# A hybrid decoder layer on 8 cores: the first tile through fp32 rows, and two weight pieces loaded in the tile before

## The chip, the cores and the metric

The kernel runs on the 8 NeuronCores of one Trainium2 chip. Each core runs the same program on its own sequence. The time is that of the device in microseconds, and the slowest core sets it. TensorE is called PE here, VectorE DVE, ScalarE ACT, GpSimd POOL, and SyncE, which only issues transfers, SP.

## The reference, cut to what matters

```python
def layer(x, c, conv_prev, g_mix, w_ada, b_ada, w_in, g_v, w_s, b_s, w_conv, w_out, g_ffn, w_ff1, w_ff2):
    mod = jax.nn.silu(c) @ w_ada + b_ada                          # (B, 6*D)
    sh1, sc1, gt1, sh2, sc2, gt2 = [m[:, None, :] for m in jnp.split(mod, N_MOD, axis=-1)]
    h = rmsnorm(x, g_mix) * (1.0 + sc1) + sh1
    p = h @ w_in                                                   # (B, T, D_IN)
    u, v, bg, cg, hin = jnp.split(p, [D_A, 2 * D_A, 2 * D_A + D_B, 2 * D_A + 2 * D_B], axis=-1)
    u = jax.nn.gelu(u)
    v = rmsnorm(jax.nn.gelu(v).reshape(bsz, t, N_HEADS_A, HEAD_DIM_A), g_v.reshape(N_HEADS_A, HEAD_DIM_A))
    a_out = u * chunk_spatial_mix(v, w_s, b_s).reshape(bsz, t, D_A)
    y_conv, new_conv = short_conv(cg * hin, conv_prev, w_conv)     # width 3, causal
    b_out = bg * y_conv
    mix = jnp.concatenate([a_out, b_out], axis=-1) @ w_out
    x = x + gt1 * mix
    h2 = rmsnorm(x, g_ffn) * (1.0 + sc2) + sh2
    f = jnp.square(jax.nn.relu(h2 @ w_ff1)) @ w_ff2
    return x + gt2 * f, v.reshape(bsz, t, D_A), new_conv
```

D_MODEL is 1024, D_A and D_B are 512, D_FF is 4096. There are 8 prompt sequences of 2048 rows and 128 single sample rows. All inputs are fp32. A core has one prompt sequence and 16 sample rows.

## The kernel before, in words

A core takes its 2048 rows in 8 tiles of 256 rows. Phase A (`tA`, the token mixer) runs over the tiles t0 to t7 and writes the new rows to a scratch tensor `x1_scr` in device memory; phase B (`tB`, the MLP) reads them back tile by tile. All weights are converted to bf16 by their transfers, which POOL issues (1024 KB in SBUF each, twice that in device memory). They are `w_ada` in 12 pieces (`ada_dma(q)`), `w_in` in the 5 groups u, v, C, h, B (`win_dma`), `w_out` in two, `w_ff1` and `w_ff2` in 8 pieces each (`ff1_dma(p)`, `ff2_dma(p)`). Rows of x and everything small are moved by transfers that SP issues. No scheduler is in play. The helper class `Sched` only records operations and adds the semaphore waits that the buffers need, so that each engine and each queue works in exactly the order in which the code is written. An engine that waits holds up all that stands behind it.

A tile of phase A goes through these steps.
- `n_load` fetches two blocks of 128 rows into buffers of the array `X`. `n_stats` squares them on ACT with a running sum, DVE scales it, and POOL takes the power of -1/2. `n_mod` multiplies the rows by that factor and by `g1B`, which is the row g_mix*(1+sc1) repeated on all partitions. `n_tr` transposes the bf16 result on PE, and ACT copies it to `hT`.
- `A_u`, `A_v` and `conv` (with `A_ch` and `A_b`) are the products with `w_in`. `A_vn` normalises v on DVE after POOL's power, and `A_spatial` is the mix within the chunk.
- `A_wout` is the product with `w_out`, four matmul groups (j, n) for a tile. DVE multiplies each by `gt1B` into one of two buffers `tmpx`, and POOL adds that onto x, which `A_reload` has fetched once more into `X[xr]`, `X[xr+1]`. SP then stores the rows to `x1_scr` (semaphores `x1s_i_j`, for tile i and block j).

The matmul results go to 8 PSUM banks, of which `next_bank` hands out 7 in turn; a bank comes free when the engine that reads it is done.

The set-up computes the modulation: `ada_cols(q)` is a product with one piece of `w_ada`, and `ada_bcast` spreads a half of sc1 over all partitions through fp32 matmuls (line 374) to make `g1B`. `setup_spatial` builds small constants on POOL and DVE and has SP copy two of them (the transfers arena<-arena). The tiles t0 to t2 are interleaved by hand in the set-up; `A_u_hold` leaves the results of u in banks until the bias is known. `wst` holds `w_s`, which POOL masks and `setup_spatial_pe` transposes. From t3 on `steady(i, mid, end, nxt, nn)` writes out a tile. It does the output products of an earlier tile `mid` before conv and of another, `end`, after it: steady(4) has t1 and t2, steady(5) has t3 and t4, steady(6) has t5, steady(7) has t6. Between the steps, `ex()` takes the next job from the list `pending`.

Several buffers of the first tiles lie where pieces 4 to 7 of `w_ff1` go later. The place of piece 4 holds X[4] and X[5], that of piece 6 holds `aT` 2 and 3 and `bT` 3 (`aT` and `bT` are the two inputs of `A_wout`).

## Time and profile before

| what | us |
|---|---|
| median of 3 runs (783.75 to 789.23) | 787.66 |
| the profiled execution, device time | 784.98 |
| its span on the slowest core, core 4 | 783.4 |
| the span of core 6, the next longest | 783.2 |
| the spans of the eight cores | 776.2 to 783.4 |
| PE busy on core 4 | 721.9 (92%) |
| PE busy in the first 92 us of core 4 | 49.86 |

The profiled execution is 1.6 us longer than the span of its slowest core and 2.7 us shorter than the median. Phase A with its set-up ends at about 313 us of the span, and the eight tiles of phase B fill the rest. Times below are microseconds from the start of the span on core 4. In the rows, a line number of a helper stands for many operations: L317 is any group of matmuls from `mm_group`, L325 any `tensor_tensor`, L328 any `scalar_tensor_tensor`, L322 any activation and L99 any transfer.

### The profile page before, as it was taken

The numbers are of one execution on the slowest core, as the hardware profiler recorded it, in microseconds if no ns is written. First come the engines' busy times: TensorE is split into PE (matmuls) and PEld (weight loads), VectorE is DVE, ScalarE is ACT, GpSimd is POOL, SyncE is SP. The second block draws the span as 40 slices with busy tenths as digits, with TensorE's granted clock in tenths as the row PEclk, the third lists the DMA queues.
The fourth block names the chain that finished last, engine by engine and source line by source line (L and its number), as shares of the span: only waits on it lengthen the run. The fifth ranks groups of instructions, "written<-read, shape, count | busy, mean of one in ns | idle before, by whom it ended". The sixth has DMA issues, their size and how long they took to land.

```text
span 783.4 us, 16529 instructions; the slowest of 8 cores (776.2 to 783.4 us)
## 1 busy us (share of the span) xinstructions
PE 721.9 (92%) x5941; PEld 498.7 (64%) x5976; DVE 373.3 (48%) x795; ACT 272.5 (35%) x560; POOL 141.8 (18%) x154
## 2 busy tenths in 40 slices
PE   1468799999999999997999999999999999999996
PEld 0354477767575766843784784774874865865854
DVE  0333667665757675440643444434433543533523
ACT  2234335423332332441441451351441531532511
POOL 5213302434544453110010000000000000000000
PEclk9989799999999999999999999999999999999998
DMA  9999999999998859997110100200200200200001
GB/s 143 186 172 168 185 187 139 172 197 247 194 275 191 201 96 208 179 192 126 67 44 26 70 18 28 82 2 28 82 1 28 82 2 27 82 1 28 28 1 55
DMA packets 46983, 83.03 MB, mean 106 GB/s; under 512 B 2204, under 2 KB 31654, under 8 KB 46902
## 3 DMA queue, kind: packets, MB, share of 16 engines
q0 software_dynamic: 32304, 36.70, 34.1%
q1 hardware_dynamic: 14598, 45.27, 18.4%
q8 instruction: 49, 0.80, 0.4%
q14 instruction: 32, 0.26, 0.1%
HBM read 101.73 MB, written 16.96 MB: 151 GB/s over the span
## 4 chain that ended last, share of the span: by engine, by line
PE 79%; DMA 14%; DVE 2%; issue 2%; ACT 1%; POOL 1%; another core or an unknown queue 0%; DVEq 0%; POOLq 0%; ACTq 0%; SPq 0%
PE ps L317 71%; DMA arena<-w_ff 6%; DMA arena<-w_ada 6%; DMA arena<-w_s 3%; PE ps L438 1%; PE ps L890 1%; ACT arena L322 1%; DVE arena L328 1%; DVE arena L325 1%; PE ps L746 1%; PE ps L583 1%; PE ps L579 1%; POOL arena L99 1%; PE ps L350 1%; PE ps L656 1%
## 5 line engine op out<-in xcount | busy, mean ns | idle before, releaser
L317 PE MATMUL ps<-arena 128*128 128x256 bf16 (+3 forms) x4376 | 635.0, 305 | 10.4 <-DVE arena L325 3.6
L317 PEld LDWEIGHTS ps<-arena 128*128 128x128 bf16 x4408 | 430.1, 98 | 205.0 <-issue 23.1
L325 POOL TENSOR_TENSOR arena<-arena 128x1 f32<-128x1 f32 (+3 forms) x100 | 107.1, 1076 | 597.1 <-DVE arena L398 466.6
L325 DVE TENSOR_TENSOR arena<-arena 128x256 bf16<-128x256 f32 (+8 forms) x354 | 159.5, 459 | 113.6 <-ACT arena L322 102.3
L322 ACT ACTIVATE arena<-ps,arena 128x256 f32<-128x256 f32 (+1 forms) x320 | 147.1, 472 | 137.4 <-PE ps L317 74.3
L322 ACT ACTIVATE arena<-arena 128x256 f32<-128x256 f32 (+4 forms) x101 | 76.8, 772 | 204.9 <-DVE arena L325 143.3
L325 DVE TENSOR_TENSOR arena<-ps,arena 128x512 f32<-128x512 f32 (+6 forms) x98 | 59.4, 610 | 179.4 <-PE ps L317 129.1
L328 DVE SCALAR_TENSOR_TENSOR arena<-arena 128x256 f32<-128x256 f32 (+4 forms) x118 | 96.2, 822 | 22.6 <-POOL arena L325 15.6
L322 ACT ACTIVATE arena<-ps 128x1024 bf16<-128x1024 bf16 (+4 forms) x86 | 50.6, 590 | 158.3 <-PE ps L438 92.1
L328 DVE SCALAR_TENSOR_TENSOR arena<-ps,arena 128x256 bf16<-128x256 f32 (+1 forms) x64 | 31.0, 484 | 23.2 <-PE ps L317 11.2
L890 PE MATMUL ps<-arena 128*128 128x512 bf16 x125 | 28.4, 379 | 5.6 <-DMA arena<-w_ff 4.8
L438 PE MATMUL ps<-arena 128*128 128x128 bf16 x256 | 20.2, 231 | 6.4 <-DVE arena L328 5.8
L890 PEld LDWEIGHTS ps<-arena 128*128 128x128 bf16 x128 | 12.0, 97 | 21.5 <-issue 8.0
L438 PEld LDWEIGHTS ps<-arena 128*128 128x128 bf16 x256 | 17.3, 103 | 9.6 <-issue 7.4
L398 DVE TENSOR_SCALAR arena<-arena 128x1 f32<-128x1 f32 x46 | 7.0, 153 | 33.1 <-ACT arena L322 32.4
L521 DVE TENSOR_REDUCE arena<-arena 128x8 f32<-128x512 f32 x16 | 10.9, 682 | 11.4 <-ACT arena L322 11.4
L350 PE MATMUL ps<-arena 128*128 128x17 bf16 x384 | 11.8, 172 | 4.9 <-DMA arena<-w_ada 4.9
L350 PEld LDWEIGHTS ps<-arena 128*128 128x128 bf16 x384 | 11.6, 98 | 5.7 <-issue 5.3
L99 POOL DMA_DIRECT2D arena<-w_ff x16 | 13.4, 840 | 9.2 <-PE ps L317 7.2
L99 POOL DMA_DIRECT2D arena<-w_ada x12 | 11.3, 941 | 10.8 <-PE ps L350 9.8
L374 PE MATMUL ps<-arena 128*128 128x128 f32 x16 | 4.1, 437 | 8.4 <-DVE arena L995 7.1
L579 PE MATMUL ps<-arena 34*128 34x512 bf16 x16 | 6.6, 412 | 5.0 <-DVE arena L1022 5.0
(86 smaller groups left out, 106.9 us busy)
## 6 DMA issues: line engine op xcount, KB each, us to landing
arena<-x_p SPq DMA_DIRECT2D x32, 512.0 KB, 11.4
arena<-w_ff POOLq DMA_DIRECT2D x16, 1024.0 KB, 36.2
arena<-w_ada POOLq DMA_DIRECT2D x12, 1024.0 KB, 44.4
x_scr<-arena SPq DMA_DIRECT2D x16, 512.0 KB, 9.6
arena<-x_scr SPq DMA_DIRECT2D x16, 512.0 KB, 4.2
y_p<-arena SPq DMA_DIRECT2D x14, 512.0 KB, 2.9
arena<-w_in POOLq DMA_DIRECT2D x5, 1024.0 KB, 64.4
arena<-w_out POOLq DMA_DIRECT2D x2, 1024.0 KB, 88.3
```

The lines of the kernel that those rows point to most:

```text
L99: fn = lambda eng, o=out, i=in_: eng.dma_start(out=o, in_=i)
L317: ins = e.matmul(out, lhsT=l, rhs=r, start=(first and i == 0), stop=(last and i == n - 1))
L322: S.op("act", lambda e: e.activation(out=out, in_=in_, func=func, **kw), reads=reads, writes=writes)
L325: S.op(eng, lambda e: e.tensor_tensor(out=out, in0=in0, in1=in1, op=op), reads=reads, writes=writes)
L328: S.op("dve", lambda e: e.scalar_tensor_tensor(out=out, in0=in0, scalar=scalar, in1=in1, op0=op0, op1=op1), reads=reads, writes=writes)
L350: ins = e.matmul(bk[:, cc * 17:(cc + 1) * 17], lhsT=ff1_v[s][:, k, cc * 128:(cc + 1) * 128], rhs=siluCT3[:, k, :], start=(k == 0), stop=(k ...
L438: ins = e.transpose(psb[:, (k - k0) * 128:(k - k0 + 1) * 128], hb[:, k * 128:(k + 1) * 128], identb)
L521: S.op("dve", lambda e: e.tensor_reduce(out=ss, in_=sqv.rearrange("p (h d) -> p h d", h=8), axis=AX.X, op=ALU.add), reads=[sqv_b], writes= ...
L579: e.matmul(bk[:, :], lhsT=indK[0:34, :], rhs=bsK[0:34, :], start=True, stop=False, skip_group_check=True)
L583: ins = e.matmul(bk[p0:p0 + 64, (h // 2) * 128:(h // 2 + 1) * 128], lhsT=vt[:, h * 64:(h + 1) * 64], rhs=wmT3[:, h, :], start=False, stop= ...
L656: ins = e.matmul(bk[:, gi * 64 + c * 16:gi * 64 + (c + 1) * 16], lhsT=w_in_g[nm][:, k, c * 128:(c + 1) * 128], rhs=hsT3[:, k, 0:16], start ...
L890: ins = e.matmul(bk[:, :], lhsT=f3[:, k, j * 128:(j + 1) * 128], rhs=wff2_v[:, k, n * 512:(n + 1) * 512], start=(k == 0), stop=(k == 31))
```

## The change

Four things are changed.

First, t0 goes another way. Its rows are multiplied in fp32 by their own factor on ACT (`first_rows`), transposed in fp32 on PE (`first_tr`, 16 transposes into 4 banks), and multiplied by g_mix*(1+sc1) when they leave the banks, where this factor is a value per partition (`first_scale`, half of it on DVE and half on ACT). t0 so needs no `g1B`.

Second, the set-up is written in another order. Both `ada_bcast` come after `ada_cols(3)`, `setup_spatial` comes after them, w_s is loaded before t2 and g_v after it without a wait, the steps n_stats and n_mod of t2 come before `ada_cols(0)`, the masking and `setup_spatial_pe` come before `ada_cols(1)`, and `ada_dma(6)` and `(7)` come after A_v of t2. A Gelu on one column is put behind the Silu.

Third, `A_v` is recorded as two operations: its 8 big matmuls no longer wait for the bias row `vbK`, only the ninth does.

Fourth, the buffers `aT` and `bT` of t4 to t7 are numbers 1, 0, 1, 0 (before 1, 2, 3, 0), and the rows of t4 are reloaded into X[2] and X[3] (before X[4] and X[5]), in steady(5) after the output product of t3 instead of before it. Pieces 6 and 4 of `w_ff1` are fetched in steady(5) (before: piece 4 in steady(6), piece 6 in steady(7)).

```diff
@@ A_v
-        S.op("pe", mm_group(bk[:, :], [(h3[:, k, j * 128:(j + 1) * 128], w_in_g["v"][:, k, :]) for k in range(8)]
-                            + [(onesK[0:34, :], vbK[0:34, :])]),
-             reads=[htb, win_b["v"], onesK_b, vbK_b], writes=[bkb])
+        S.op("pe", mm_group(bk[:, :], [(h3[:, k, j * 128:(j + 1) * 128], w_in_g["v"][:, k, :]) for k in range(8)], last=False),
+             reads=[htb, win_b["v"]], writes=[bkb])
+        S.op("pe", mm_group(bk[:, :], [(onesK[0:34, :], vbK[0:34, :])], first=False), reads=[onesK_b, vbK_b], writes=[bkb])
@@ AI: the number of aT and bT
-        return (tl["i"] + 1) % 4
+        return (1, 2, 3, 0, 1, 0, 1, 0)[tl["i"]]
@@ tA
-    ... xr=(4, 2, 4, 2, 4, 2, 2, 2)[i],
+    ... xr=(4, 2, 4, 2, 2, 2, 2, 2)[i],
@@ set-up
+    act(bF[:, 0:1], mhalf[:, 0:1], AF.Gelu_apprx_tanh, [mhalf_b], [bF_b[0]])
...
-    for j in range(2):
-        n_stats(tA[0], j)
-    setup_spatial()
+    def first_rows(tl):
+        for j in range(2):
+            n_stats(tl, j)
+        for j in range(2):
+            xt, xb, _ = X[tl["x"] + j]
+            rs, rs_b = tl["rs"][j]
+            act(xt, xt, AF.Copy, [xb] + rs_b, [xb], scale=rs)
+    XT_BANKS = (5, 6, 7, 2)
+    def first_tr(tl):
+        for q, b in enumerate(XT_BANKS):
+            bk, bkb = banks[b]
+            def fn(e, bk=bk, q=q):
+                ins = None
+                for kk in range(2):
+                    for j in range(2):
+                        k = 2 * q + kk
+                        ins = e.transpose(bk[:, kk * TILE + j * 128:kk * TILE + (j + 1) * 128], X[tl["x"] + j][0][:, k * 128:(k + 1) * 128], identf)
+                return ins
+            S.op("pe", fn, reads=[X[tl["x"]][1], X[tl["x"] + 1][1], identf_b], writes=[bkb])
+    def first_scale(tl, hf):
+        h3, htb = h3_of(tl)
+        m, mb = modT[1]
+        bk, bkb = banks[XT_BANKS[2 * hf + 1]]
+        k0 = 4 * hf + 2
+        tt("dve", h3[:, k0:k0 + 2, 0:TILE], bk.rearrange("p (k t) -> p k t", k=2), m[:, k0:k0 + 2, 16:17].broadcast_to([128, 2, TILE]),
+           ALU.mult, [bkb, mb], [htb])
+        bk, bkb = banks[XT_BANKS[2 * hf]]
+        for kk in range(2):
+            k = 4 * hf + kk
+            act(h3[:, k, 0:TILE], bk[:, kk * TILE:(kk + 1) * TILE], AF.Copy, [bkb, mb], [htb], scale=m[:, k, 16:17])
+    ring[0] = (0, 1)
+    first_rows(tA[0])
     ada_cols(2)
-    ada_bcast(2, g1B, g1B_b, col, col_b)
+    first_tr(tA[0])
+    first_scale(tA[0], 0)
...
     ada_cols(3)
+    first_scale(tA[0], 1)
+    ada_bcast(2, g1B, g1B_b, col, col_b)
     ada_bcast(3, g1B, g1B_b, col, col_b)
     q3_in = landed(ff1_b[ADA_SLOT[3]])
-    q1_in = landed(ff1_b[ADA_SLOT[1]])
-    for j in range(2):
-        n_mod(tA[0], j)
+    setup_spatial()
@@ loads of the set-up and t0 to t2
     for j in range(2):
         n_load(t1, j, after=[q3_in])
+    load(wst3, w_s.rearrange("h t s -> t h s"), wst_b, "wst", after=[win_b["u"]])
     for j in range(2):
-        n_load(t2, j, after=[win_b["u"]])
-    load(gvB, g_v.partition_broadcast(128), [gvB_b], "gvB", after=[q1_in])
-    load(wst3, w_s.rearrange("h t s -> t h s"), wst_b, "wst")
-    for j in range(2):
-        n_tr(t0, j)
+        n_load(t2, j)
+    load(gvB, g_v.partition_broadcast(128), [gvB_b], "gvB")
     A_u_hold(t0, hold[0])
...
@@ steady
-        if end is not None:
+        if end is not None and i < 5:
             reload(end)
...
         if mid is not None:
             wout(mid)
+        if end is not None and i == 5:
+            reload(end)
@@ pending
-        lambda: s_v2(),
+        lambda: (s_v2(), ff1_dma(6)),
...
-        lambda: s_zout(ncs[:, 512:1024].rearrange("t (c n) -> t c n", c=4)),
+        lambda: (s_zout(ncs[:, 512:1024].rearrange("t (c n) -> t c n", c=4)), ff1_dma(4)),
...
-        lambda: ff1_dma(4),
+        None,
         lambda: s_mod(x1sT, x1sT_b, 4, 3),
-        None, None,
-        lambda: ff1_dma(6),
```

Where the instructions now stand can be seen in three places.

DVE in the set-up, the changed kernel from the set-up's second `ada_cols` on (L325 with 128x68 and L328 belong to it, L325 with 128x512 is the second half of `first_scale`, the two L367 are the columns of the two `ada_bcast`, L965 to L970 are `setup_spatial`):

```order
L325 TENSOR_TENSOR arena<-ps1,arena 128x68 [waits c_pe,c_act]
L328 SCALAR_TENSOR_TENSOR arena<-arena 128x68 [waits c_dve]
L325 TENSOR_TENSOR arena<-ps2,arena 128x512 [waits c_dve]
L367 COPY arena<-arena 128x512
L367 COPY arena<-arena 128x512 [waits c_dve,c_pe]
L965 CAST arena<-arena 2x128 [waits c_pool]
L967 CAST arena<-arena 2x512 [waits d_bsrow,c_pool]
```

Before, the casts L965 to L970 stood ahead of both `ada_cols` on DVE; now they stand behind the second column copy, which waits for PE.

SP in the set-up, before and after as one piece (x_p are rows of t1 and then of t2; d_ff1w1 is piece 3 of `w_ada`, d_ff1w3 piece 1; ahead of this piece stand the two copies of `setup_spatial`, arena<-arena, each with a wait for DVE, in both kernels):

```order
 L99 DMA arena<-x_p 128x1024 [waits d_ff1w1]
 L99 DMA arena<-x_p 128x1024
-L99 DMA arena<-x_p 128x1024 [waits d_win_u,d_X0,c_act,c_dve]
-L99 DMA arena<-x_p 128x1024 [waits d_X1,c_act,c_dve]
-L99 DMA arena<-g_v 128x512 [waits d_ff1w3]
-L99 DMA arena<-w_s 128x8x128
+L99 DMA arena<-w_s 128x8x128 [waits d_win_u]
+L99 DMA arena<-x_p 128x1024 [waits c_act,c_pe]
+L99 DMA arena<-x_p 128x1024 [waits c_act]
+L99 DMA arena<-g_v 128x512
```

w_s moved ahead of t2 and away from the wait for piece 1 of `w_ada`; the loads of t1 kept their place behind the two copies.

SP in steady(5) and steady(6), before and after as one piece (x_p with a wait for x1s_i_j is a reload that waits until the store of tile i, block j has landed; x1_scr<-arena are the stores of t3 and further down of t4):

```order
-L99 DMA arena<-x_p 128x1024 [waits d_x1s_2_0]
-L99 DMA arena<-x_p 128x1024 [waits d_x1s_2_1]
 L99 DMA x1_scr<-arena 128x1024 [waits c_pool] x2
+L99 DMA arena<-x_p 128x1024 [waits d_x1s_3_0]
+L99 DMA arena<-x_p 128x1024 [waits d_x1s_3_1]
 L99 DMA ncs<-arena 16x4x128 [waits c_dve]
 L99 DMA mod_scr<-arena 8x128 [waits c_dve]
 L99 DMA x1_scr<-arena 128x1024 [waits c_pool] x2
-L99 DMA arena<-x_p 128x1024 [waits d_x1s_3_0]
-L99 DMA arena<-x_p 128x1024 [waits d_x1s_3_1]
+L99 DMA arena<-x_p 128x1024 [waits d_x1s_4_0]
+L99 DMA arena<-x_p 128x1024 [waits d_x1s_4_1]
```

The reload of t4 now stands behind the stores of t3 and waits for them, and that of t5 waits for the stores of t4 instead of those of t3.

## Rows read from the trace of the kernel before

**Rows 1.** The page: clock and DMA share in tenths, 40 slices of the span.

```profile
PEclk9989799999999999999999999999999999999998
DMA  9999999999998859997110100200200200200001
```

**Rows 2.** Chain that ended last, first 140 us: start, length, what.

```profile
6.14 44.50 DMA arena<-w_ada
...
51.09 20.74 DMA arena<-w_s
```

**Rows 3.** Timeline of the first 135 us: start, length, engine, line [idle before <-releaser].

```profile
21.32 3.41 SPq L99 DMA_DIRECT2D arena<-arena  x2
24.83 10.44 SPq L99 DMA_DIRECT2D arena<-x_p  x4
29.47 2.04 PE L374 MATMUL ps<-arena 128*128 128x128 f32 x8 [1.34 <-DVE arena L367]
37.45 5.81 PE L317 MATMUL ps<-arena 128*128 128x256 bf16 x32 [1.43 <-ACT arena L322]
46.08 3.65 PE L317 MATMUL ps<-arena 128*128 128x256 bf16 x32 [1.93 <-ACT arena L322]
67.93 8.45 PE L317 MATMUL ps<-arena 128*128 128x512 bf16 x35 [1.94 <-DVE arena L325]
82.70 0.58 PE L579 MATMUL ps<-arena 34*128 34x512 bf16 x1 [4.98 <-DVE arena L1022]
85.29 6.23 PE L317 MATMUL ps<-arena 128*128 128x512 bf16 x17 [0.33 <-issue]
131.66 0.96 PE L350 MATMUL ps<-arena 128*128 128x17 bf16 x32
```

**Rows 4.** Stretches of 2 us, PE alone: busy, instructions, clock, DMA share, GB/s.

```profile
76.00:78.00 2.00, 1.72 (x12) 1.00 1.15 158
80.00:82.00 2.00, 0.00 (x0) 0.50 1.18 170
```

**Rows 5.** Transfer of piece 6 of w_ada: its issue, then us to landing.

```profile
73.00 1.80 POOL L99 DMA_DIRECT2D arena<-w_ada  x2
...
arena<-w_ada POOLq DMA_DIRECT2D x1, 1024.0 KB, 54.7
```

**Rows 6.** Stores of t3, the adds before them, and DVE in t5, t6.

```profile
225.11 2.97 SPq L99 DMA_DIRECT2D x_scr<-arena  x2
242.04 0.69 DVE L325 TENSOR_TENSOR arena<-ps,arena 128x512 f32<-128x512 f32 x1 [1.10 <-PE ps L317]
258.48 0.69 DVE L325 TENSOR_TENSOR arena<-ps,arena 128x512 f32<-128x512 f32 x1 [1.17 <-PE ps L317]
255.78 1.26 POOL L325 TENSOR_TENSOR arena<-arena 128x512 f32<-128x512 f32 x1 [3.62 <-DVE arena L325]
```

**Rows 7.** Us to landing: stores of 225.1, 258.9; loads of 247.3, 297.8, 216 to 218.5.

```profile
x_scr<-arena SPq DMA_DIRECT2D x1, 512.0 KB, 11.0
x_scr<-arena SPq DMA_DIRECT2D x1, 512.0 KB, 5.2
arena<-x_p SPq DMA_DIRECT2D x1, 512.0 KB, 7.7
arena<-x_p SPq DMA_DIRECT2D x1, 512.0 KB, 9.9
arena<-x_p SPq DMA_DIRECT2D x1, 512.0 KB, 14.6
```

**Rows 8.** Stretches of 10 us: busy of PE, PEld, DVE, ACT, POOL; clock, DMA share, GB/s.

```profile
240.00:250.00 10.00, 10.00 (x106) 5.33 (x105) 7.00 (x9) 2.46 (x4) 7.02 (x5) 1.00 0.76 180
280.00:290.00 10.00, 9.95 (x66) 5.96 (x65) 6.71 (x12) 3.66 (x7) 8.62 (x8) 1.00 0.38 49
```

**Rows 9.** Waits of PE, 130 to 420 us: core 4, then core 6.

```profile
PE ps L890 <- DMA arena<-w_ff: 4.8, 3, 2.6
...
PE ps L890 <- DMA arena<-w_ff: 4.1, 2, 2.3
```

More of the change, by code:

```diff
@@ L900, in build_nc @@
     NT = SEQ // TILE
-    tA = [dict(kind="A", i=i, w=TILE, row0=i * TILE, x=(2 if i in (1, 3) else 0), h=(0, 1, 2, 0, 1, 0, 1, 0)[i], xr=(4, 2, 4, 2, 4, 2, 2, 2)[i],
+    tA = [dict(kind="A", i=i, w=TILE, row0=i * TILE, x=(2 if i in (1, 3) else 0), h=(0, 1, 2, 0, 1, 0, 1, 0)[i], xr=(4, 2, 4, 2, 2, 2, 2, 2)[i],
                x1b=bufs("x1s_%d_0" % i, "x1s_%d_1" % i)) for i in range(NT)]
@@ L1035, in build_nc @@
     hold = {0: (3, 4), 1: (5, 6)}
-    ring[0] = (0, 1, 2, 7)
     for j in range(2):
         n_load(t1, j, after=[q3_in])
+    load(wst3, w_s.rearrange("h t s -> t h s"), wst_b, "wst", after=[win_b["u"]])
     for j in range(2):
-        n_load(t2, j, after=[win_b["u"]])
-    load(gvB, g_v.partition_broadcast(128), [gvB_b], "gvB", after=[q1_in])
-    load(wst3, w_s.rearrange("h t s -> t h s"), wst_b, "wst")
-    for j in range(2):
-        n_tr(t0, j)
+        n_load(t2, j)
+    load(gvB, g_v.partition_broadcast(128), [gvB_b], "gvB")
     A_u_hold(t0, hold[0])
+    ring[0] = (0, 1, 2, 7)
     for j in range(2):
@@ L1052, in build_nc @@
     A_u_hold(t1, hold[1])
+    for j in range(2):
+        n_stats(t2, j)
+    S.op("pool", lambda e: e.affine_select(out=wst3, in_=wst3, compare_op=ALU.is_ge, fill=0.0, base=0,
+                                           pattern=[[0, 8], [-1, 128]], channel_multiplier=1), reads=wst_b, writes=wst_b)
+    for j in range(2):
+        n_mod(t2, j)
     ada_cols(0)
@@ L1055, in build_nc @@
     for j in range(2):
-        n_stats(t2, j)
-    for j in range(2):
-        n_mod(t2, j)
-    for j in range(2):
         n_tr(t2, j)
-    S.op("pool", lambda e: e.affine_select(out=wst3, in_=wst3, compare_op=ALU.is_ge, fill=0.0, base=0,
-                                           pattern=[[0, 8], [-1, 128]], channel_multiplier=1), reads=wst_b, writes=wst_b)
+    setup_spatial_pe()
     ada_cols(1)
@@ L1072, in build_nc @@
         A_u(t2, c)
-    for q in (6, 7):
-        ada_dma(q)
     load(xS, x_s.rearrange("t (k n) -> (t k) n", k=8), [xS_b], "xS", after=[win_b["C"]])
@@ L1086, in build_nc @@
         A_v(t1, j)
-    setup_spatial_pe()
     for j in range(2):
@@ L1093, in build_nc @@
         A_v(t2, j)
+    for q in (6, 7):
+        ada_dma(q)
     for j in range(2):
```

## The prediction

> **What bounds the kernel now.** Start with the page [rows 1]: the clock row shows two dips, in slices 3 and 5 (about 40 to 100 us), and the DMA row stands at 9 for the first 12 slices, to 235 us. PE is busy 49.86 of the first 92 us and nearly all the time afterwards. So only three places are left where an edit of order can gain: the set-up, the point where phase A ends, and whatever wait the change itself makes. I read them in that order.
>
> In the set-up, the chain of waits [rows 2] names the transfer of the last early piece of `w_ada` (to 50.6 us) and then w_s, which SP issues at 51.09, only after that piece, and which lands at 71.8. The timeline [rows 3] shows what hangs on it: the spatial product of t0 starts at 82.70 after PE has waited 4.98 us. That wait takes the clock along: it is 1.00 at 76 us and 0.50 (1.2 GHz of 2.4) at 80 us [rows 4]. The 17 matmuls of A_v(t2) behind it take 6.23 us, where 17 at the rate of the 35 before it (8.45 us) would take 4.1 [rows 3]: 2.1 us is this trace's price of one such cold stretch.
>
> At the end of phase A, PE waits 4.8 us in three waits for pieces of `w_ff2` on core 4, and 4.1 on core 6 [rows 9]. There the transfers are late, not PE.
>
> Between 100 and 340 us PE hardly waits. Nothing is to be won there; whatever the change adds there is lost. The DMA share is 1.0 to 1.1 until 240 us, then 0.76, and 0.38 at 280 to 290 us [rows 8]: there is some room late in phase A, and it is into this room that the two pieces of `w_ff1` are moved.
>
> **The set-up.** t0 no longer waits for `g1B`, but both `ada_bcast` still stand ahead of its u product on PE. Piece 3 lands at about 24 us; `ada_cols(3)`, which now stands behind the 16 fp32 transposes, ends near 26; DVE then scales, copies the first column at 28, PE takes 2.04 us for each cast [rows 3], the second copy waits for the first cast, and the second cast ends near 33. A_u_hold(t0) starts there instead of 37.45 [rows 3]: 4.5 us won at this point.
>
> What is lost stands on SP. The two copies of `setup_spatial` are issued at 21.32 and 24.15, the rows of t1 at 24.83 [rows 3]. These copies need DVE casts which now stand behind the second column copy, so near 31.5 and 34. The loads of t1 are queued behind them and leave at about 34.7, 10 us later, and w_s, t2 and g_v follow in one heap. With the 9.9 us that a load takes on full DMA queues [rows 7], t1 is there at 44.6 and 46.5. Squares, power, `n_mod` (1.28 us a block) and transposes add 6 to 7 us, and A_u_hold(t1) starts near 53 instead of 46.08, cold again, since PE had 10 us with nothing to do: 5.8 us instead of 3.65 [rows 3]. Through t2, `ada_cols(1)` and the bias of u, I come to A_v(t0) at 71.5, 3.6 us later than 67.93; 1.9 of what it would be later is given back because A_v no longer waits for `vbK` (its wait there is 1.94 [rows 3]), and 1.3 by the table load that is now done early.
>
> From there the order pays. A_v of t0 and t1 takes 8.45 us, to 80. The mask, the transposes of w_s and the copy at line 1022 are done long before; the power for t0 is no longer queued behind two `ada_dma`. The spatial product of t0 waits for v alone and starts near 80.3, 0.4 us after A_v(t1), too little to lose the clock. 1.4 us for it and 4.1 for A_v(t2) give 85.8 instead of 91.5: 5.7 us ahead.
>
> Not all of it survives. Piece 6 of `w_ada` is issued at 73.0 and lands 54.7 us later, at 127.7 [rows 5]; its product starts at 131.66 [rows 3]. Transfers issued by POOL are served in order, and the bytes ahead of this piece are the same in the changed kernel, so PE cannot be more than 4.0 us ahead there. **Term 1: -4.0 us.** Its bounds are 0 (t1 and t2 land 5 us later than I think) and -4.8 (less other traffic ahead of piece 6).
>
> **The end of phase A.** Piece 6 of `w_ff1` is issued at 291 us today, in the middle of the pieces of `w_ff2`; it lands after 25.4 us and takes some 10 us of the queue. Moved to steady(5), it frees these 10 us, while PE needs the last pieces only 4.8 earlier: all waits go. What is late next is PE itself. On core 4 that is 4.8 us, but core 6 (span 783.2) waited 4.1 [rows 9], and 783.2 - 4.1 = 779.1 is the slowest core then. **Term 2: -4.3 us**, with bounds of 0 and -4.8.
>
> **Tiles 5 and 6.** This is the part that costs. t4's rows used to be fetched into X[4] and X[5], free long before. Now X[2] is taken: t3's sum must be added, stored and landed before t4 can be fetched, and t5 comes behind t4 in the same buffer. In times of the kernel before: the store of t3 is issued at 225.1 and lands 11.0 us later [rows 6, 7], at 236.1. The reload then takes 9.9 (a load on full queues) or 7.7 (at share 0.76) [rows 7, 8]. The queues will be full: two more pieces stand ahead, and a piece takes 10 us or more there, so the room after 240 us is used up until about 275. I take 9.9: t4 is there at 246.0.
>
> POOL needs 1.26 us for an add [rows 6]. DVE has two buffers `tmpx`, so its third multiply of t4 waits for the first add, to 247.3 instead of 242.04 [rows 6]. PE does not feel this: the banks that it needs next are free. But the store of t4 can only go at 248.7. With 11.0 and 9.9 once more, t5 is there at 269.6, its first add ends at 270.9, and the third multiply of t5, at 258.48 today [rows 6], ends at 271.6. Behind it on DVE stands the whole of conv(t6). PE has five small groups after its output product of t5 (the square sum of the sample rows, a transpose, C, H, C), to about 263.3; the sixth needs the bank that the third multiply reads. PE stands still from 263.3 to 271.7, 8.4 us, which is longer than the 4.98 that brought the clock down in the set-up, so I add the same 2.1. SP, too, waits with the loads of tB[0] behind the reload of t5; ACT squares these late in conv(t6), with 1 us to spare or short of it. **Term 3: +10.5 us.** Its lower bound is nothing: with 5.2 for a store and 7.7 for a load the third multiply of t5 would not be held beyond 262. Its upper bound uses 14.6, the slowest class of load [rows 7], for both loads: t4 at 250.7, t5 at 279.0, the multiply done at 281, a stall of 17.7 and with the clock 19.8.
>
> One rule of the Trainium skill bears on this ("DMA: Bandwidth & Descriptors", section on queues, rings and completion order): each DMA engine takes packets in turn from the queues that have work. By it, a longer heap of weight pieces would not make a single reload slower, only the time of full queues longer. That is how I use 9.9 and 11.0, and the first of these rows was taken with `w_ff2` pieces in the heap.
>
> **Edits that cost nothing.** aT and bT in turns of two: t5 writes number 0 after the output product of t3 has read it, earlier on the same engine. The early issue of pieces 6 and 4 costs POOL nothing new. The fp32 transposes (3.5 to 4.3 us cold, an estimate from the 2.04 us of four fp32 products) are hidden while piece 3 is on its way; without that cover they would cost this much.
>
> **Sum.** -4.0 - 4.3 + 10.5 = +2.2 us. The profiled execution (784.98, its span 783.4) would become 787.2; the median, 2.7 above it, 787.66 + 2.2 = **789.9 us**.
>
> **Rivals.**
> The reload chain is hidden. If transfers are served faster, or the earlier pieces are through before 250 us, term 3 falls to 0 to 4. For it: at 247 us loads landed in 7.7, at 258.9 a store in 5.2 [rows 7]. Against it: these rows are from the room that the change fills. Time: 787.66 - 8.3 = 779.4 at best, 781 as its middle. Chance 0.24.
> The front gains nothing. The late rows of t1 and t2 eat all of the 5.7 us. For it: 10 us of delay at SP are sure from the order of instructions. Against: the wait at 82.70 and the cold stretch go for certain. Time: 793.9. Chance 0.12.
> The pieces of `w_ff2` stay late, so that moving piece 6 does not do what it is for, because they are issued late themselves (three at 313 us and after). Against: they land one after the other 5 to 10 us apart, as in a heap. Time: 794.2. Chance 0.05.
> The slow end: one mechanism, the chain of store, reload, add, store, reload for t3, t4 and t5. It decides from the point at which both legs together take more than about 16 us each round (the forecast has 20.9); at 25.6 the stall is 17.7 and the sum 19.8 - 8.3 = +11.5: 799 us, or 797 as its middle. For it: burst loads at 216 us took 14.6 [rows 7]. Chance 0.13.
>
> **How the numbers follow.** The forecast holds 0.46 and reaches from 785 to 794. A change of 1% (7.9 us) is about what a measurement of this kernel can tell from none. Below 779.8 lies half of the first rival, 0.12. Above 795.5 lies most of the slow end and a little of the second and third, 0.15. Between them 0.73. The range, 780 to 797, leaves out half of the first rival and a part of the last.
>
> **What the profile after would show.** Right: A_u_hold(t0) at about 33 us; rows of t1 issued on SP near 35 and a gap of PE near 40 to 49 us; no wait at the spatial product of t0 and the clock at 1.00 there; the product with piece 6 of `w_ada` near 127.7; no waits for `w_ff2`; a gap of PE of 6 to 10 us in conv(t6), ended by DVE, which was held by POOL, which waited for x_p. Wrong: if the rows of t1 are issued near 25, if no gap stands in conv(t6), or if stores and reloads in tiles 5 and 6 land within 7 us, the gain is larger than I say; if a second gap stands behind the reload of t4 in tile 5, it is smaller.

## The result and the profile after

The changed kernel takes 793.9 us (median of 6 runs, 793.06 to 798.79); the kernel before, run beside it, 785.85 (6 runs, 783.48 to 789.23). The ratio is 1.0108, with a 95% interval of 1.0084 to 1.0132: 8.5 us slower (1.08% of 787; the two medians differ by 8.05). The forecast was 2.2 us slower, or 789.9 us from a kernel before at 787.66. Some executions fall in a slower state of the chip, in which the cores of one die or both show a lower granted clock; medians, ratios and differences here are over the others alone. The profiled execution of after is the slowest of its six (798.79 us), so single waits in it may be longer than usual. Its cores span 786.5 to 797.2 us, with granted clocks of 0.967 to 0.977; before they were 0.982 to 0.987.

The page of after, the rows that answer [rows 1]:

```profile
span 797.2 us, 16579 instructions; the slowest of 8 cores (786.5 to 797.2 us)
...
PEclk9966999999899999999999999999999999999998
DMA  9999997999999938998030020200200200200001
```

Before, the clock stood at 8 in slice 3 and 7 in slice 5; now it is 6 in slices 3 and 4 (40 to 80 us): more of the set-up is cold, not less. A shallow dip is at slice 11 (about 200 us).

**The set-up.** Timeline of after, core 2, first 100 us, PE; the columns are start, length, engine, line, form and count, then the idle time before and what ended it. Answers to [rows 3]:

```profile
31.06 5.67 PE L317 MATMUL ps<-arena 128*128 128x256 bf16 x32
47.38 1.01 PE L438 MATMUL ps<-arena 128*128 128x128 bf16 x8 [10.65 <-DVE arena L328]
...
51.33 5.75 PE L317 MATMUL ps<-arena 128*128 128x256 bf16 x32 [1.32 <-ACT arena L322]
56.91 0.96 PE L350 MATMUL ps<-arena 128*128 128x17 bf16 x32
62.86 1.01 PE L438 MATMUL ps<-arena 128*128 128x128 bf16 x8 [4.99 <-DVE arena L328]
65.41 1.01 PE L438 MATMUL ps<-arena 128*128 128x128 bf16 x8 [1.54 <-DVE arena L325]
...
71.68 16.25 PE L317 MATMUL ps<-arena 128*128 128x256 bf16 x76
88.25 0.37 PE L579 MATMUL ps<-arena 34*128 34x512 bf16 x1 [0.31 <-issue]
...
97.84 1.75 PE L465 MATMUL ps<-arena 128*128 128x2 bf16 x64
```

Read it downwards. A_u_hold of t0 starts at 31.06 instead of 37.45 (near 33 was forecast). It runs cold: its 32 products take 5.67 us, where the same 32 take 3.65 at full clock (46.08 in [rows 3]). Then PE waits 10.65 us for the rows of t1 (L438 is the transposes) and 4.99 more for those of t2. The spatial product of t0 (L579) has lost its wait of 4.98, but comes at 88.25 instead of 82.70. The last row, the bias products of C and h, is my mark for the end of the set-up: 97.84 here, 96.8 to 99.5 over the cores; before it stood at 90.3 to 92.7 (91.4 in the mean, against 98.1). **The set-up is 5 to 7 us longer**, where 5.7 less were forecast at this point and 4.0 less behind piece 6 of w_ada. The loss stays: the product with piece 6 starts at 136.87 on core 2 (near 127.7 was forecast, 131.66 before on core 4), and the first L621, a small product of the sample rows, at 148.98, against 143.77 before on core 4.

Why t1 and t2 are late can be read in SP's queue, core 2, same columns:

```profile
29.27 2.73 SPq L99 DMA_DIRECT2D arena<-arena  x2
32.10 0.86 SPq L99 DMA_DIRECT2D arena<-x_p  x2
33.05 0.57 SPq L99 DMA_DIRECT2D arena<-w_s  x1
33.78 6.79 SPq L99 DMA_DIRECT2D arena<-x_p  x2
```

The two copies of `setup_spatial` go out at 29.3 instead of 21.3, and t1 behind them at 32.1 instead of 24.8 [rows 3]. Between t1 and t2 stands w_s. The transfers issued in these rows, us from issue to landing (w_s, then the first block of t2), and ACT's first square of t2:

```profile
arena<-w_s SPq DMA_DIRECT2D x1, 512.0 KB, 22.1
arena<-x_p SPq DMA_DIRECT2D x1, 512.0 KB, 23.4
57.33 1.06 ACT L322 ACTIVATE arena<-arena 128x1024 bf16<-128x1024 f32 x1 [6.15 <-DMA arena<-x_p]
```

w_s has the bytes of a block of x, in rows of 512 bytes instead of 4096, and takes 22 us; the block of t2 queued behind it takes 23.4 where the two of t1, ahead of w_s, take 10.9 in the median and 9.9 was forecast. The clock, in stretches of 2 us of core 2 (busy time of PE, PEld, DVE, ACT, POOL; clock; DMA share; GB/s), answering [rows 4]:

```profile
44.00:46.00 2.00, 0.00 (x0) 0.00 (x0) 0.40 (x2) 1.15 (x2) 0.45 (x2) 0.50 1.12 178
52.00:54.00 2.00, 2.00 (x11) 1.43 (x10) 0.00 (x0) 0.00 (x0) 0.00 (x0) 0.50 1.10 279
72.00:74.00 2.00, 2.00 (x12) 1.23 (x11) 0.74 (x5) 1.53 (x4) 0.00 (x0) 0.50 1.20 178
```

PE fell to 1.2 GHz in the wait for t1, and again in the one for t2, so that A_u of t2 too begins cold.

**Tiles 5 and 6.** The chain that ended last, core 2 (start, length, what), is the one that the prediction drew:

```profile
233.10 11.21 DMA x_scr<-arena
244.37 12.04 DMA arena<-x_p
259.30 8.85 DMA x_scr<-arena
268.20 7.65 DMA arena<-x_p
278.19 3.23 PE ps L317 x16
```

Store of t3, reload of t4, store of t4, reload of t5, then PE. POOL and PE in the timeline (POOL of core 2, PE of core 2, PE of core 6):

```profile
275.99 8.17 POOL L325 TENSOR_TENSOR arena<-arena 128x512 f32<-128x512 f32 x5 [7.95 <-DMA arena<-x_p]
278.19 3.23 PE L317 MATMUL ps<-arena 128*128 128x256 bf16 x16 [3.06 <-DVE arena L325]
275.32 3.26 PE L317 MATMUL ps<-arena 128*128 128x256 bf16 x16 [6.07 <-DVE arena L325]
```

The gap in conv(t6) is there on four cores (2, 3, 0 and 6: 3.06, 3.12, 4.10 and 6.07 us), and on the other four not at all.

**The end of phase A.** No core of after waits for w_ff2; the first products with it (L890) run through on core 2 (against 4.8 and 4.1 us of waits in [rows 9]):

```profile
357.28 25.23 PE L890 MATMUL ps<-arena 128*128 128x512 bf16 x112
```

**One thing that no step spoke of.** On cores 1, 2, 3, 4 and 7 PE pauses in tile 4, amid the short products of the sample rows (L656), with nothing to wait for, and runs on cold. Core 2:

```profile
201.58 0.39 PE L656 MATMUL ps<-arena 128*128 128x16 bf16 x9 [4.20 <-issue]
201.82 7.35 PE L317 MATMUL ps<-arena 128*128 128x256 bf16 x48
```

The same 48 products take 5.40 us on core 6, which has no pause. In the profiled execution of before no core has it.

### The profile page after: what moved, and what is told of

Its sections match the earlier page's. It is cut to its first block, busy times and chain, and to the rows that moved or that the text cites. A ratio compares the mean times of both kernels' runs of the same rounds, so it can differ in the third digit from the quotient of the medians.

```text
span 797.2 us, 16579 instructions; the slowest of 8 cores (786.5 to 797.2 us)
## 1 busy us (share of the span) xinstructions
PE 731.6 (92%) x5976; PEld 503.4 (63%) x5976; DVE 370.9 (47%) x795; ACT 274.9 (34%) x565; POOL 142.9 (18%) x154
## 4 chain that ended last, share of the span: by engine, by line
PE 68%; DMA 16%; DVE 4%; issue 4%; POOL 3%; ACT 2%; SPq 1%; DVEq 0%; POOLq 0%; ACTq 0%
PE ps L317 60%; DMA arena<-x_p 11%; DMA x_scr<-arena 4%; POOL arena L325 3%; PE ps L890 3%; ACT arena L322 2%; DVE arena L325 2%; DVE arena L328 2%; SPq L99 1%; DMA mod_scr<-arena 1%; PE ps L438 1%; PE ps L746 1%; PE ps L1009 0%; PE ps L465 0%; DVE arena L521 0%
## 5 line engine op out<-in xcount | busy, mean ns | idle before, releaser
L317 PE MATMUL ps<-arena 128*128 128x256 bf16 (+2 forms) x4408 | 643.6, 307 | 8.9 <-DVE arena L325 6.4
L317 PEld LDWEIGHTS ps<-arena 128*128 128x128 bf16 x4408 | 431.9, 99 | 208.4 <-issue 23.3
L325 POOL TENSOR_TENSOR arena<-arena 128x1 f32<-128x1 f32 (+3 forms) x100 | 108.5, 1089 | 631.6 <-DVE arena L398 464.3
L325 DVE TENSOR_TENSOR arena<-arena 128x256 bf16<-128x256 f32 (+8 forms) x354 | 159.5, 459 | 112.4 <-ACT arena L322 102.5
L322 ACT ACTIVATE arena<-ps,arena 128x256 f32<-128x256 f32 (+1 forms) x324 | 149.0, 472 | 148.1 <-PE ps L317 72.3
L322 ACT ACTIVATE arena<-arena 128x1024 bf16<-128x1024 f32 (+5 forms) x104 | 79.3, 773 | 229.8 <-DVE arena L325 142.9
L325 DVE TENSOR_TENSOR arena<-ps,arena 128x512 f32<-128x512 f32 (+6 forms) x100 | 60.7, 611 | 180.0 <-PE ps L317 120.7
L328 DVE SCALAR_TENSOR_TENSOR arena<-arena 128x256 f32<-128x256 f32 (+4 forms) x116 | 94.9, 823 | 19.2 <-POOL arena L325 15.3
L322 ACT ACTIVATE arena<-ps 128x16 f32<-128x16 f32 (+4 forms) x84 | 48.5, 580 | 133.6 <-PE ps L438 76.6
L328 DVE SCALAR_TENSOR_TENSOR arena<-ps,arena 128x256 bf16<-128x256 f32 (+1 forms) x64 | 31.0, 484 | 22.7 <-ACT arena L322 9.2
L438 PE MATMUL ps<-arena 128*128 128x128 bf16 x240 | 18.8, 231 | 17.9 <-DVE arena L328 16.2
L438 PEld LDWEIGHTS ps<-arena 128*128 128x128 bf16 x240 | 16.2, 103 | 21.1 <-issue 18.9
L890 PE MATMUL ps<-arena 128*128 128x512 bf16 x128 | 28.4, 379 | 0.4
L890 PEld LDWEIGHTS ps<-arena 128*128 128x128 bf16 x128 | 12.2, 98 | 16.0 <-issue 2.0
L521 DVE TENSOR_REDUCE arena<-arena 128x8 f32<-128x512 f32 x16 | 10.9, 682 | 7.4 <-ACT arena L322 7.3
L322 ACT ACTIVATION_READ_ACCUMULATOR arena<-arena 128x1 f32 x51 | 9.6, 188 | 0.0
L579 PE MATMUL ps<-arena 34*128 34x512 bf16 x16 | 6.1, 383 | 2.8 <-DVE arena L325 1.7
```

Of the source, the lines that this page charges most:

```text
L317: ins = e.matmul(out, lhsT=l, rhs=r, start=(first and i == 0), stop=(last and i == n - 1))
L322: S.op("act", lambda e: e.activation(out=out, in_=in_, func=func, **kw), reads=reads, writes=writes)
L325: S.op(eng, lambda e: e.tensor_tensor(out=out, in0=in0, in1=in1, op=op), reads=reads, writes=writes)
L328: S.op("dve", lambda e: e.scalar_tensor_tensor(out=out, in0=in0, scalar=scalar, in1=in1, op0=op0, op1=op1), reads=reads, writes=writes)
L438: ins = e.transpose(psb[:, (k - k0) * 128:(k - k0 + 1) * 128], hb[:, k * 128:(k + 1) * 128], identb)
L521: S.op("dve", lambda e: e.tensor_reduce(out=ss, in_=sqv.rearrange("p (h d) -> p h d", h=8), axis=AX.X, op=ALU.add), reads=[sqv_b], writes= ...
```

## The experiments

My theory for the size: the set-up loses time, through SP's queue. The rival: the loss is made in tiles 5 and 6, as forecast, or in the pause at L656. Gains and losses in us are the ratio less 1, times 787. The mark "bias products" is the row at 97.84 above, over the eight cores of a run.

**The two halves apart.** e1_front_only is the changed kernel with everything of tiles 4 to 7 put back; e2_back_only is the kernel before with exactly that.

```
e1: -        return (1, 2, 3, 0, 1, 0, 1, 0)[tl["i"]]     xr=(4, 2, 4, 2, 2, 2, 2, 2)
    +        return (tl["i"] + 1) % 4                     xr=(4, 2, 4, 2, 4, 2, 2, 2)
    (reload(end) and pieces 6 and 4 of ff1 at their old places)        e2: the reverse, in before
```

> The changed kernel with everything of tiles 4 to 7 put back (buffers, reload, pieces of w_ff1 as before); the set-up and A_v stay changed. Theory 1, the set-up itself is slower, because the rows of t1 and t2 come late: the two bias products that follow the spatial product of t1 start near 98 us instead of 91 to 92.7, and all of it stays, so 5 to 6 us slower than the kernel before (791). PE again waits 3 to 5 us for pieces of w_ff2. Theory 2, the loss is in tiles 4 to 7 alone: within 1.5 us of the kernel before (786).

> The kernel before with only the changes of tiles 4 to 7 (aT and bT numbers, t4 reloaded into X[2] after the store of t3, pieces 6 and 4 of w_ff1 in tile 5). Theory 1: a gap of PE of 3 to 8 us in conv(t6) on most cores, no waits for w_ff2, together 1 to 5 us slower than before (787 to 791). Theory 2, all of the loss is here: 8 us slower (794).

e1: 792.59 us, ratio 1.0083 (1.0058 to 1.0109), +6.5 us; bias products 96.4 to 99.2. e2: 788.53, ratio 1.0038 (1.0021 to 1.0055), +3.0 us, no wait for w_ff2. Together 1.21%, against 1.08% for the whole change. The waits for w_ff2 in e1 add up to 3.7 us on core 4 and to less on the others. So two thirds of the loss are the set-up, the part that was to gain. In e2 the gap in conv(t6) is on core 3 alone:

```profile
268.92 3.57 PE L317 MATMUL ps<-arena 128*128 128x256 bf16 x16 [5.00 <-DVE arena L325]
```

**The second half taken apart.** e3_bufs_only: the buffers and the reloads as changed, the pieces of ff1 at their old places. e4_piece6_only: t4's rows stay in X[4]; only aT and bT in turns of two, and piece 6 in tile 5.

```
e3: before with  AI (1, 2, 3, 0, 1, 0, 1, 0), xr[4] = 2, reload(end) of tile 5 behind wout(mid)
e4: before with  AI (1, 2, 3, 0, 1, 0, 1, 0) and
    -        lambda: s_v2(),
    +        lambda: (s_v2(), ff1_dma(6)),
    (and no ff1_dma(6) at its old place)
```

> The kernel before with the buffers and the late reload of t4, but the pieces of w_ff1 fetched where they were. It tells the chain of store and reload from the load of the two earlier pieces. If the chain costs by its length alone (11.0 and 9.9 us a leg), conv(t6) has the same gap as in e2 and the kernel is 3 to 8 us slower than before. If the gap needs the full queues that the two pieces make, it is below 2 us here and the kernel within 2 us of before. In both cases PE waits 3 to 5 us for w_ff2.

> The kernel before with the new numbers of aT and bT and piece 6 of w_ff1 fetched in tile 5; piece 4, X[4] and the reload of t4 stay as they were. If the wait for w_ff2 is what moving piece 6 takes away, and no other cost comes with it: 3.8 to 4.3 us faster (about 782), no gap in conv(t6). If a piece more in the queue of tile 5 costs by itself (reloads late, PE held by POOL): no gain or a loss.

e3: 785.9, ratio 0.9986 (0.9962 to 1.001), and no gap in conv(t6) on any core; the waits for w_ff2 are 2.1 us at most (core 2), not the 3 to 5 that I expected. e4: 786.0, ratio 0.9992 (0.9972 to 1.0012), and no wait for w_ff2. So neither the chain of reloads alone nor the early piece 6 alone costs anything that can be measured; the loss of e2 needs the one buffer and the early pieces together. It differs from e4 by 0.46%, 3.6 us. And the waits for w_ff2, once gone, do not give back the 4.3 us that I had entered.

**The kernel before once more**, for the pause at L656, unchanged (so no diff).

> The kernel before once more, unchanged, for one more profile. All four runs so far, but not the first profile of the kernel before, show on some cores a pause of PE of 1.2 to 4.2 us inside the sample rows' product of tile 4 (line 656), with no releaser in the trace. If it is chance from execution to execution, it stands here on some cores too. If it belongs to the changed kernels, no core shows it here.

786.64 us, and the pause is there on cores 2, 6 and 7 (1.66, 3.52, 3.24 us); core 7, then core 6:

```profile
192.35 0.33 PE L656 MATMUL ps<-arena 128*128 128x16 bf16 x7 [3.24 <-issue]
191.71 0.34 PE L656 MATMUL ps<-arena 128*128 128x16 bf16 x7 [3.52 <-issue]
```

Always the same spot: 7 products before the end of a row of 96 (9 in the changed kernel). Which cores have it changes from execution to execution, and it is no work of the change; the execution that the prediction was made from had simply been spared. The other marks move too: the bias products stand at 88.2 to 93.8 here.

**The two orders on SP.** e6_setup_early is e1 with `setup_spatial()` right behind `ada_cols(2)`, ahead of the fp32 transposes. e7_setup_early_ws_last also loads t2 ahead of w_s.

```
e6:      ada_cols(2)
    +    setup_spatial()
         first_tr(tA[0])
         ...
         q3_in = landed(ff1_b[ADA_SLOT[3]])
    -    setup_spatial()
e7: -    load(wst3, ..., "wst", after=[win_b["u"]])
         for j in range(2):
    -        n_load(t2, j)
    +        n_load(t2, j, after=[win_b["u"]])
    +    load(wst3, ..., "wst")
```

> The front of the changed kernel (e1) with setup_spatial moved up behind the first ada_cols, so that SP can issue the rows of t1 at about 25 us instead of 32; w_s still stands ahead of t2 on SP. Theory 1a, the loss of the front is the two copies ahead of t1: most of the 6.6 us comes back, bias products at 91 to 93 us, time within 1.5 us of before (786). Theory 1b, the loss is w_s ahead of t2 (22 us to landing, t2 behind it): t2 lands at 55 us or later still, bias products at 96 or later, still 4 us or more slower than before (790).

> As e6, and the rows of t2 stand ahead of w_s on SP, issued once the u weights have landed, as in the kernel before; w_s and g_v follow without the wait for piece 1 of w_ada. Both theories of the front: t2 lands near 45 us, w_s near 57, no wait of PE over 2 us at the spatial product of t0, bias products at 84 to 88 us. PE then meets piece 6 of w_ada, which lands near 127 us, so no more than 4 us faster than before (782).

e6: 786.43, ratio 1.0007 (0.9984 to 1.0029): 6.0 us of e1's 6.5 are back by the place of one call. Bias products 90 to 93.4 (mean 91.7), as before the change. The rows of t1 go out at 24.62, and the loss that is left is the one behind w_s, core 1:

```profile
42.31 3.65 PE L317 MATMUL ps<-arena 128*128 128x256 bf16 x32 [1.78 <-ACT arena L322]
...
58.67 1.01 PE L438 MATMUL ps<-arena 128*128 128x128 bf16 x8 [11.91 <-DVE arena L328]
```

e7: 783.52, ratio 0.9965 (0.9934 to 0.9996), bias products 85 to 87.4 (mean 86.3), 5 us ahead of before. The wait of 11.91 is gone; PE now waits for w_s itself, core 2:

```profile
48.82 0.61 PE L438 MATMUL ps<-arena 128*128 128x128 bf16 x8 [1.19 <-DVE arena L325]
55.52 1.94 PE L1052 MATMUL ps<-arena 128*128 128x128 f32 x8 [6.09 <-POOL arena L1090]
```

Most of the 5.7 us of lead that the prediction wanted is there, and piece 6 of w_ada does not cut it to 4.0: its product starts at 125.60 on core 4 (131.66 before), with no wait. But only 2.8 arrive at the end: waits for w_ff2 are back on three cores (1.4 to 1.5 us), and seven of eight cores pause at L656.

**The gains together.** e8_best is e7 with the edits of e4.

> e7 with piece 6 of w_ff1 fetched in tile 5 and the new numbers of aT and bT, piece 4 and X[4] as before (e4). If the two gains add: the 4 us of e7 and the 3.4 us of waits for w_ff2 that e4 lost (with a time that stayed equal), so 779 to 782. If e4's result holds, nothing beyond e7.

782.26 us, ratio 0.9944 (0.9921 to 0.9968), 4.4 us faster than before. Five cores pause at L656, by up to 4.66 us. The slowest span is 781.2; the three cores without the pause are through in 770 to 772.

**The pause.** e9_best_spread is e8, and e10_before_spread the kernel before, with the five groups of 32 short products each in a job of its own.

```
-        ada_job(8, D1(0)),
-        lambda: [s_win(g) for g in range(2)],
-        ada_job(9, D1(1)),
-        lambda: ([s_win(g) for g in range(2, 5)], s_elem1(), s_v1()),
-        lambda: ada_row(4),
+        lambda: (ada_job(8, D1(0))(), s_win(0)),
+        lambda: s_win(1),
+        lambda: (ada_job(9, D1(1))(), s_win(2)),
+        lambda: s_win(3),
+        lambda: (s_win(4), s_elem1(), s_v1(), ada_row(4)),
```

> This is the fastest version so far (the set-up with its two copies ahead of the rows of t1 and the rows of t2 ahead of w_s; aT and bT in turns of two; piece 6 of w_ff1 in tile 5), with one edit: the five groups of 32 short products of the sample rows at line 656 (two groups and then three in one row of 96) each get a job of their own, with large products between them. In all kernels so far, the unchanged one too, PE pauses for 1.2 to 4.7 us on some cores at the same spot, 7 or 9 products before the end of the row of 96, with no releaser ('issue'), and the clock falls behind it. Theory C: the row of 96 products of some 27 ns uses up PE's instructions faster than they are delivered; with at most 32 in a row no core pauses over 0.5 us at line 656 or behind it, the slowest span falls from 781.2 to 772 to 774, and the median from 782.8 to 775 to 778. Rival D: the delivery is late at this stretch of the program (180 to 195 us) whatever the kind of instruction; some cores then still pause for 1 to 5 us between 180 and 200 us, at line 317 or 656, and the median stays at 781 to 784.

> The kernel before with the same one edit (the five groups of line 656 in jobs of their own). Theory C: no pause over 0.5 us near 188 us on any core. The profiled execution of before that the prediction was made from had none of these pauses, the second one had them on 3 cores (1.66, 3.52, 3.24), among them the slowest core; so C gives 0 to 5 us less than before, 781 to 785, ratio 0.993 to 1.000. Rival D: pauses on about 3 cores, ratio 1.000. If the spread products cost by themselves (the stationary operand is loaded for 16 columns, with nothing to gain from their place), the ratio is over 1.000, by 1 us at most.

No core pauses in either (none of 16; e8 and e5 together had it on 8 of 16). e9, core 5, around the spot:

```profile
188.67 0.95 PE L656 MATMUL ps<-arena 128*128 128x16 bf16 x32
189.48 5.40 PE L317 MATMUL ps<-arena 128*128 128x256 bf16 x48
...
197.02 0.95 PE L656 MATMUL ps<-arena 128*128 128x16 bf16 x32
```

e9 takes 779.87 us, ratio 0.9906 (0.9881 to 0.9931), 7.4 us faster than before and 3.0 faster than e8 (these two intervals overlap). e10: 783.57, ratio 0.9966 (0.995 to 0.9982), 2.7 faster. Theory C, that a long row of short products outruns the delivery of PE's instructions, foretold that the pause goes with the length of the row; the last section shows the transfer that PE waits for. e9's median missed the 775 to 778 that I had given; the slowest span is 778.4, not 773, since other small waits have come (2.33 us at L317 on core 2). That the edit is worth about as much in both (3.0 and 2.7) suggests that the pause is little or no part of the 8.5 us between before and after; on the changed kernel itself it was not tried.

**Is the set-up of the change needed at all?** e11_before_ws_early swaps two lines in the kernel before: w_s is loaded ahead of g_v. e12_best_mask_late is e9 with the transposes of w_s back behind A_v of t1.

```
e11: +    load(wst3, ..., "wst")
          load(gvB, ..., after=[q1_in])
     -    load(wst3, ..., "wst")
e12: -    setup_spatial_pe()      (behind n_tr(t2, j))
          ...
              A_v(t1, j)
     +    setup_spatial_pe()
```

> The kernel before with two lines swapped: the load of w_s ahead of the load of g_v, so that it no longer waits for piece 1 of w_ada but is issued right behind the rows of t2. Theory A (the set-up of the change is not needed for its gain): the wait of 4.98 us at the spatial product of t0 and the cold stretch behind it go, the bias products of C and h come at 86 to 88 instead of 92.7, and the rows of t1 are issued near 25 as before. The lead that is left at the product with piece 6 of w_ada is 4 us at most: median 782 to 784, ratio 0.995 to 0.998. Rival B: the lead goes into waits for w_ff2 and for piece 6 of w_ada, ratio 0.999 to 1.001. Rival: w_s, with its small rows, slows the rows of t2 or a piece of w_in, and the bias products stay at 91 or later.

> e9 with the transposes of w_s (line 1052, in setup_spatial_pe) moved back behind A_v of t1, where the kernel before has them. In e7 PE waited 6.09 us there for the mask on POOL, which waits for w_s. Theory: that wait goes, little comes in its place, and the bias products of C and h come at 82 to 85 instead of 85.5 to 88.7; if the lead survives, the median is 2 to 3 us below e9. Rival: the product with piece 6 of w_ada, which lands when it lands, takes the lead: e9's time within 1 us.

e11: 786.37, ratio 0.9979 (0.9959 to 0.9999), at the edge of what can be told from nothing. The wait for w_s is gone and another has taken its place at the spatial product, on all eight cores (core 7 is shown), so that the bias products come at 88.9 to 92.6 and not at 86 to 88:

```profile
81.97 0.58 PE L579 MATMUL ps<-arena 34*128 34x512 bf16 x1 [3.62 <-ACT arena L322]
```

e12: 786.14, ratio 0.9994 (0.9978 to 1.001): all of e9's gain is lost, and both my theories for it are wrong. The bias products come at 90.7 to 98.4 (mean 95.5), in e9 at 85.5 to 90.1 (mean 88.2). Core 3; the last row is ACT:

```profile
59.32 1.01 PE L350 MATMUL ps<-arena 128*128 128x17 bf16 x32 [8.91 <-DMA arena<-w_ada]
...
67.19 16.23 PE L317 MATMUL ps<-arena 128*128 128x256 bf16 x76 [4.75 <-ACT arena L322]
...
88.49 0.45 PE L579 MATMUL ps<-arena 34*128 34x512 bf16 x1 [3.74 <-ACT arena L322]
...
62.80 4.24 ACT L322 ACTIVATE arena<-ps,arena 128x256 bf16<-128x256 f32 x8 [10.60 <-DVE arena L470]
```

Without the transposes in front, PE waits 8.91 us for piece 1 of w_ada, which lands when it lands (near 59; in e9 PE waits 7.15 us for the mask and 2.06 for this piece, on core 5). So they cost nothing in the changed place. In the old place the copies of w_s stand in ACT's queue behind the work on v, and the spatial product waits for them: 3.74, and 3.62 in e11. The wait of 4.98 "for DVE L1022" [rows 3] thus had a second one right behind it; on cores 3 and 7 of before it is the one that the profile names, with 3.62.

The 4.75 us at 67.19 stand on all eight cores and are a side effect of the edit, in the order of the banks. `setup_spatial_pe` takes three banks from `next_bank`. With it gone from there, the count of the calls in kernel.py gives bank 6 to the first group of A_u(t2), instead of bank 2. Bank 6 holds results of A_u_hold(t1), and ACT empties the held banks in order: its eight activations end at 67.04, and PE goes on at 67.19. So e12 does not test the place of the transposes alone.

## Why the prediction was right or wrong, step by step

**The step that failed is Term 1, the set-up: -4.0 forecast, +6.5 measured (e1).** Three parts of it went wrong. (1) The delay of t1 was seen and sized well: rows issued near 35 forecast, at 32.10 in the trace; A_u_hold(t1) near 53 forecast, at 51.33. What failed is the stretch behind it: from A_u_hold(t1) to A_v(t0) the forecast allows 18.5 us (53 to 71.5), and the trace takes about 28 (51.33 to near 79; 21.9 in before). (2) The load of t2 was sized wrong. I took the load of t2 as one of a heap at 9.9 us, and wrote that w_s, t2 and g_v "follow in one heap", when the trace of before already had w_s at 20.74 [rows 2]. With w_s ahead of it, t2 landed at 57.2; PE waited 4.99 more and was cold again. e7 sets the price of this order: from a mean of 91.7 in e6 to 86.3 at the bias products, 5.4 us, of which 3.3 are left at the end (0.9965 against 1.0007). (3) I let one cold stretch of 5.8 us stand for the whole, where the clock was 0.50 through most of 42 to 76 us. With that, A_v(t0) was not at 71.5 but near 79, and the gain behind it could not make it good: the wait of 4.98 was gone on all cores, but the cold stretch behind it on five of eight only. On cores 1, 4 and 5 the clock fell to 0.50 between 90 and 92 us all the same, although PE's idle time just ahead (1.3 us) is that of the other cores. The lower side of the bound, "0 (t1 and t2 land 5 us later than I think)", was right in its condition and wrong in its sum: a bound of nothing was set where the same condition gives a loss.

The cause was named, though: "what is lost stands on SP". Putting the two copies back ahead of t1 (e6) gives 6.0 us. And the cap on the gain, "PE cannot be more than 4.0 us ahead" at piece 6 of w_ada, was wrong as well: in e7 PE is 6.1 us ahead there (125.60 and 131.66 on core 4) and does not wait, although POOL issues the piece at 90.14 instead of 73.00.

**Term 2, the end of phase A: -4.3 forecast, -0.6 measured** (e4: 0.9992, an interval that holds 1). The waits are gone on all cores: from the second L621 to the end of the last L890, e4 takes 108.2 to 109.3 us, before 109.5 to 113.8. But the price was read from two cores of one execution: in the second one of before (e5) this stretch takes 108.2 to 111.7 us, and only core 7 has such a wait above 1.2 us. Five cores of e4 pause at L656, so that a part of the gain may lie under that.

**Term 3, the reload chain: +10.5 forecast, about +3.6 measured** (e2 less e4). The mechanism is as forecast, row by row. From the issue of the store of t3 to the landing of t5 the forecast has 44.5 us, the trace 42.5 to 43.9 on the four cores with a gap (on core 2 from 233.10 to 275.9, 42.8), and 38.5 to 39.1 on the four without. What was off is the start. In the trace of before, the add ahead of that store had itself waited for its reload, core 4:

```profile
222.36 5.33 POOL L325 TENSOR_TENSOR arena<-arena 128x512 f32<-128x512 f32 x4 [5.35 <-DMA arena<-x_p]
```

so that the store left 22.5 us ahead of the product at L727; in after, on core 2, it leaves 26.4 ahead (233.10 and 259.54). These 3.9 us of room turn the stall of 8.4 into 4.5, and the chain, 1.7 shorter than forecast, into 2.8: core 2 shows 3.06. On core 6 the same sum (24.4 ahead, 43.9 for the chain) gives 5.9, and the trace 6.07. The clock's price of 2.1 was near: from the second L621 to the single product at L1293 the cores with a gap take 58.8 to 62.0 us and those without 54.1 to 54.6, which leaves 1.5 us (core 6) to 3.8 (core 0) beside the gap. That the chain needs the two early pieces, as I argued, is shown by e3: without them, no gap.

The prediction drew on the rule that each DMA engine takes packets in turn from the queues that have work (the Trainium skill, "DMA: Bandwidth & Descriptors", section on queues, rings and completion order), and read from it that a longer heap does not make a single reload slower. The reloads here do not speak against it: 12.0 and 7.7 us against the 9.9 used. The same section of the Trainium skill says that on each DMA engine descriptors are taken in the order of the ring, and it is this sentence, not the other, that bore on t2 behind w_s, whose 23.4 us agree with it.

**The sum.** +2.2 forecast, +8.5 measured. By parts: front +6.5 instead of -4.0; tiles 4 to 7 +3.0 instead of +6.2. The errors have opposite signs. That 793.9 us still lies in the range of 780 to 797 is luck in part: two errors offset each other, and the kernel before ran at 785.85 beside it, not at 787.66. The rival "the front gains nothing" (793.9) gave the measured time by luck: it held the forecast of tiles 5 and 6, which was too high, against a front that lost instead of gaining nothing.

**The edits said to cost nothing.** aT and bT in turns of two: nothing to see in e3 and e4. The fp32 first tile: A_u_hold(t0) is 6.4 us earlier than before in the changed kernel, but with SP's copies back in front (e6) the bias products are only where they were before; it may pay in e7, where t1 and t2 are there in time, but no run has e7's order of loads without it. Its 16 transposes take 3.65 us (19.99 on core 2), and the product with piece 3 follows them with no wait, so that how much of them was hidden cannot be told.

**What stays open.** Which parts of the changed set-up the gain of e7 needs: the fp32 first tile, the order of the transposes of w_s and the split of A_v were never tried apart. How often the pause at L656 comes, and whether an earlier PE makes it more frequent (seven cores in e7, three in e5). Piece 4 early with t4 in its own buffer was not tried, since the piece needs that space.

## What to carry to other kernels

When a set-up step is moved, follow its DMAs first: here two copies of 0.5 and 2 KB, moved behind DVE work, held the rows of the next tile for 7 us and cost 6 us at the end. In a queue that is served in order, place by the time to landing of what stands ahead, and put what is needed last at the end; w_s ahead of t2 cost 5.4 us at the end of the set-up, and the other order is part of a kernel (779.9 us) that beats both. And before a wait is used as a price, look at a second execution and at all cores: a wait that moves from core to core is worth less than its length, and a trace that happens to be free of a pause hides one. Where operations take banks in turn, moving one moves the banks of all that follow: in e12 that alone made a wait of 4.75 us.
